# Bias rows of a modulation projection folded into its partial sums, and two of its chunks summed earlier

## The reference, cut to what matters

```
mod_l = split(silu(c) @ ada_w[i] + ada_b[i], 6)      # ada_w[i]: 1024 x 6144
h  = rmsnorm(x, norm_mix_g[i]) * (1 + mod_l[1]) + mod_l[0]
x  = x + mod_l[2] * mixer(h)
f  = rmsnorm(x, norm_ffn_g[i]) * (1 + mod_l[4]) + mod_l[3]
x  = x + mod_l[5] * grouped_moe(f)
```

## Time and profile before

| | us |
|---|---|
| three runs | 1031.48, 1037.86, 1030.33 (median 1031.48) |
| profiled execution | 1036.62, span of the trace 1034.8 |
| PE busy | 781.3 (76% of the span) |
| DVE busy | 392.3 (38%) |
| ACT busy | 178.6 (17%) |
| POOL busy | 28.0 (3%) |
| mean granted TensorE clock | 0.853 of full speed |

### The profile page before, as it was taken

How to read it: one execution, slowest core, us unless ns; L and a number is a source line. 1 busy time by engine, 2 the same in 40 slices (tenths; PEclk the granted TensorE clock), 3 DMA queues, 4 the chain that set the end, 5 groups by cost and what they waited for, 6 DMA issues and landing times.

```text
span 1034.8 us, 18303 instructions
## 1 busy us (share of the span) xinstructions
PE 781.3 (76%) x6820; PEld 433.2 (42%) x6821; DVE 392.3 (38%) x883; ACT 178.6 (17%) x381; POOL 28.0 (3%) x43
## 2 busy tenths in 40 slices
PE   3989899997959549976669953596478878798580
PEld 1534647544544225543235521272344444354240
DVE  2267879647978642120112101623512111121013
ACT  3211011115530201110111100420111111111001
POOL 0000000020000010000000001000000000000001
PEclk9899999799989669996779976799599898799785
DMA  9887988789507788589999899902789899999923
GB/s 346 297 300 254 343 296 286 274 303 320 213 1 269 302 342 346 215 350 415 418 417 414 337 416 396 404 20 102 294 307 365 325 416 417 414 417 415 415 82 127
DMA packets 102222, 320.53 MB, mean 310 GB/s; under 512 B 12315, under 2 KB 27547, under 8 KB 85667
## 3 DMA queue, kind: packets, MB, share of 16 engines
q1 hardware_dynamic: 78454, 282.88, 69.9%
q0 software_dynamic: 3952, 21.37, 5.4%
q10 hardware_dynamic: 19776, 15.75, 4.7%
HBM read 303.58 MB, written 24.64 MB: 317 GB/s over the span
## 4 chain that ended last, share of the span: by engine, by line
PE 30%; issue 27%; DVE 14%; DMA 13%; SPq 11%; ACT 1%; POOL 1%; ACTq 1%; DVEq 0%; POOLq 0%
PE bank L1469 7%; SPq L492 6%; DMA raw<-in_w_up 5%; DMA arena<-unit_rows 5%; PE bank L1678 3%; PE bank L1602 3%; PE bank L1785 3%; PE bank L1473 2%; DVE arena L873 2%; DMA arena<-in_ada_b 2%; PE bank L1691 2%; PE bank L1459 1%; PE bank L1478 1%; SPq L457 1%; DMA bias<-in_ada_b 1%
## 5 line engine op out<-in xcount | busy, mean ns | idle before, releaser
L1678 PE MATMUL bank<-raw,arena 128*32 128x256 f32 x3392 | 251.6, 441 | 73.2 <-DMA raw<-in_w_up 41.5
L1678 PEld LDWEIGHTS bank<-raw,arena 128*32 128x32 f32 x3392 | 120.5, 124 | 184.0 <-DMA raw<-in_w_up 57.1
L1285 DVE TENSOR_TENSOR arena<-arena,bank 64x256 f32<-64x256 f32 x53 | 22.5, 425 | 345.8 <-ACT arena L784 345.8
L1691 PE MATMUL bank<-raw,arena 128*32 128x256 f32 x1696 | 112.7, 393 | 0.8 <-DVE arena L1273 0.8
L1691 PEld LDWEIGHTS bank<-raw,arena 128*32 128x32 f32 x1696 | 60.8, 115 | 40.3 <-issue 5.6
L1469 PE MATMUL bank<-ring,arena 128*128 128x512 f32 x160 | 72.3, 611 | 0.0
L873 DVE SCALAR_TENSOR_TENSOR bias<-ring,small,bias 128x512 f32<-128x512 f32 x84 | 63.2, 752 | 3.0
L1665 PE MATMUL bank<-consts_sb,arena 64*128 64x64 f32 x212 | 37.0, 298 | 33.8 <-DVE arena L1285 17.2
L784 ACT ACTIVATE arena<-bank 64x256 f32<-64x256 f32 x53 | 19.9, 376 | 237.8 <-PE bank L1678 219.2
L1665 PEld LDWEIGHTS bank<-consts_sb,arena 64*128 64x128 f32 x212 | 29.4, 198 | 43.9 <-issue 23.6
L1469 PEld LDWEIGHTS bank<-ring,arena 128*128 128x128 f32 x160 | 31.2, 196 | 39.0 <-issue 39.0
(11 more groups left out here) (229 smaller groups left out, 792.5 us busy)
## 6 DMA issues: line engine op xcount, KB each, us to landing
raw<-in_w_gate SPq DMA_DIRECT2D x64, 1024.0 KB, 18.5
raw<-in_w_up SPq DMA_DIRECT2D x64, 1024.0 KB, 20.6
raw<-in_w_down SPq DMA_DIRECT2D x64, 1024.0 KB, 22.0
ring<-in_ada_w SPq DMA_DIRECT2D x24, 2048.0 KB, 13.3
ring<-in_w_in SPq DMA_DIRECT2D x7, 2048.0 KB, 10.9
unit_results<-arena ACTq DMA_DIRECT2D x244, 32.0 KB, 7.1
arena<-unit_rows ACTq DMA_DIRECT2D x55, 128.0 KB, 6.9
ring<-in_w_out SPq DMA_DIRECT2D x2, 2048.0 KB, 32.8
```

The source lines that it names most:

```text
L1678: ins = mm(ps[4][o:o + S, 0:FW], xT[:, i, j * S:(j + 1) * S], w[:, k % 4, h * FW:(h + 1) * FW], start=(k == 0), stop=(k == KD - 1))
L1691: ins = mm(ps[5][j * S:(j + 1) * S, 0:XW], hT_e[:, k % QN, k // QN * S:(k // QN + 1) * S], w[:, k % 2, j * XW:(j + 1) * XW], start=(k == 0 ...
```

## The change

The bias rows of layer 2's chunks are now loaded in the stream like those of layer 1, into a second two-row tile `bias1` that lies where the DFT constants go later, and every chunk's first pass starts from it. The three bias transfers and the three additions between the layers are gone. Chunks 20 and 21 are summed behind steps 21 and 22, ahead of the attention loop; 22 and 23 stay behind it. The fills stay behind chunk 19's save. At the passage, SP issues the three transfers of sums first, then the DFT constants (before: at the end of the stream), then waits for the results, and only then loads `w_fnet`. ACT makes eight of the twelve copies ahead of its squares and four behind them.

```diff
-ADA_AFTER = {n: 4 + i for i, n in enumerate((0, 2, 4, 5, 6, 7, 8, 9, 11, 12, 14, 16, 17, 18, 19, 20))}
-FILL_AFTER = 4 + len(ADA_AFTER) - 1
+ADA_AFTER = {n: 4 + i for i, n in enumerate((0, 2, 4, 5, 6, 7, 8, 9, 11, 12, 14, 16, 17, 18, 19, 20, 21, 22))}
+FILL_AFTER = 19
+MODS_FIRST = 8
+        bias1 = cst("dft").rearrange("p (b n) -> p b n", b=2)
...
             def load_bias(c):
                 if c >= 6:
                     sp.wait_ge(acc_ready, c - 5)
-                sp.dma_start(bias[0:1, c % 2, :], adab[0:1, c * W:(c + 1) * W]).then_inc(bias_in[c % 2], 16)
+                l, at = c // N_ADA, c % N_ADA * W
+                sp.dma_start((bias, bias1)[l][0:1, c % 2, :], adab[l:l + 1, at:at + W]).then_inc(bias_in[c % 2], 16)
...
-                if n and STREAM[n - 1][0] == "ada" and 4 <= STREAM[n - 1][1] < N_ADA:
+                if n and STREAM[n - 1][0] == "ada" and STREAM[n - 1][1] >= 4:
                     load_bias(STREAM[n - 1][1])
...
-            sp.dma_start(K_[:, K_PARTS[2]:K_PARTS[3]], consts[:, K_PARTS[2]:K_PARTS[3]]).then_inc(dft_in, 16)
...
-            sp.wait_ge(L[0]["expert_closed"], NE - 2)
+            sp.wait_ge(L[0]["expert_closed"], NE - 1)
+            for p in range(3):
+                sp.dma_start(mods[:, AT1[2 * p]:AT1[2 * p] + 2, :].rearrange("p a (b n) -> p (a b) n", b=2),
+                             scratch[4 * p:4 * p + 4].rearrange("c p n -> p c n")).then_inc(acc_back[p], 16)
+            sp.dma_start(K_[:, K_PARTS[2]:K_PARTS[3]], consts[:, K_PARTS[2]:K_PARTS[3]]).then_inc(dft_in, 16)
+            for t in range(TT):
+                sp.wait_ge(y_back[t], 32)
             for hf in range(2):
                 sp.dma_start(slot(FNET_AT + hf), fnet_v[:, :, hf * W:(hf + 1) * W]).then_inc(fnet_in[hf], 16)
-            sp.wait_ge(L[0]["expert_closed"], NE - 1)
-            for p in range(3):
-                load_sums(sp, p)
-            for t in range(TT):
-                sp.wait_ge(y_back[t], 32)
...
-            for n in range(N_ADA):
+            for n in range(MODS_FIRST):
                 mod1_copy(n)
             norm2(3, lambda t: act.wait_ge(added, t + 1))
+            for n in range(MODS_FIRST, N_ADA):
+                mod1_copy(n)
...
+            nc.vector.memset(bias1, 0.0).then_inc(bias_zero, 1)
...
                 for k in range(KD):
-                    if k == 0 and c >= N_ADA:
-                        ins = nc.vector.tensor_scalar(acc, w[:, k, :], cc[:, k:k + 1], None, ALU.mult)
-                    else:
-                        ins = nc.vector.scalar_tensor_tensor(acc, w[:, k, :], cc[:, k:k + 1],
-                                                             bias[:, c % 2, :] if k == 0 else acc, ALU.mult, ALU.add)
+                    first = (bias, bias1)[c // N_ADA][:, c % 2, :]
+                    ins = nc.vector.scalar_tensor_tensor(acc, w[:, k, :], cc[:, k:k + 1], first if k == 0 else acc,
+                                                         ALU.mult, ALU.add)
...
-                    if c < N_ADA:
-                        dve.wait_ge(bias_in[c % 2], 16 * (c // 2 - 1))
+                    dve.wait_ge(bias_in[c % 2], 16 * (c // 2 - 1))
...
-            for p in range(3):
-                add_bias1(p)
...
-                pe.wait_ge(bias1_added, c // 4 + 1)
                 pe.wait_ge(acc_back[c // 4], 16)
```

More of the change, by code:

```diff
@@ L339, in program @@
         gain_late = sem("gain_late")
-        bias1_added = sem("bias1_added")
-        acc_back, bias1_in = ([sem(f"{n}{p}") for p in range(3)] for n in ("acc_back", "bias1_in"))
+        acc_back = [sem(f"acc_back{p}") for p in range(3)]
         acc_saved = [sem(f"acc_saved{b}") for b in range(2)]
@@ L416, in program @@
         MOD1_ORDER = [2, 3, 0, 1] + list(range(4, N_ADA))
[L418 to L427, removed]
         @block.sync
@@ L466, in _ @@
                 if n == 4:
-                    sp.wait_ge(bias_zero, 1)
+                    sp.wait_ge(bias_zero, 2)
                     sp.dma_start(K_[:, K_PARTS[1]:K_PARTS[2]], consts[:, K_PARTS[1]:K_PARTS[2]]
@@ L857, in _ @@
             dve.wait_ge(silu_c, 1)
-            dve.wait_ge(bias_zero, 2)
+            dve.wait_ge(bias_zero, 3)
             nc.vector.tensor_tensor(c_pair[:, :, 0:2], cc.rearrange("p (w k) -> p k w", w=2),
@@ L1346, in combine_results @@
                     ins.then_inc(added, 1)
[L1348 to L1353, removed]
             residual(0, [0, 1, 2, 3], mod0[:, 0, :])
```

## The result

The changed kernel takes 1045.47 us (median of four runs, 1044.34 to 1046.18) against 1033.78 us for the kernel before (four runs, 1030.33 to 1037.86): ratio 1.0103, 95% interval 1.0076 to 1.0131. It is 11.7 us slower (1.0%). The forecast was +12.2 us and 1043.7 us, counted from 1031.48, the median of the three runs known then.

What follows compares the result with a forecast made beforehand. Serial chains were taken to bound the kernel: before the attention, and sums and biases between the layers. Terms 25.2 - 12.95 = +12.2 us on the median 1031.48 gave 1043.7 us, eight in ten from 1023 to 1052.

Steps and rivals of the forecast that it cites:

- The wait of chunk 21: Ahead of the attention: chunk 21's bias row, behind chunk 22's load, lands at 255.7; decay rows on DVE +25.2 us.
- Chunk 20: Ahead of the attention: its bias row follows chunk 21's load, so it runs from about 226.8 to 233.0.
- The rest of the stream at nothing: SP's other loads, held back one or two entries by the added bias rows, stay hidden: 0 us.
- Shorter work behind the attention and earlier weights at nothing: Behind the attention: two chunks fewer on DVE and 4 MB of expert weights sooner give 0 us.
- The passage: Between the layers: results fetch becomes the latest wait, DVE's mean at 650.7 instead of 663.65, -12.95 us.
- The total: Whole kernel: 25.2 - 12.95 = +12.2 us, for a median 1043.7 us; forecast as summed given 0.60.
- The rival with completion out of order: Ahead of the attention: chunk 21's row gets through the fills, 1021.0 us; chance 0.13 before 243, 0.10 to 252.

Runs made afterwards that it cites:

- the move alone: Kernel before with chunks 20 and 21 summed ahead of the attention, fills behind chunk 19's save, nothing folded, passage as before: 1033.89 us, ratio 1.0010.
- the variant with the rows first: Changed kernel with bias rows of chunks 20 and 21 issued just ahead of the loads of chunks 21 and 22: 1021.58 us, ratio 0.9909.

## Why the prediction was right, point by point

**The wait of chunk 21: right.** The row was taken to land 1.2 us ahead of chunk 22's load, at 255.7; it landed at 253.8, 2.1 us ahead of 255.9. Delay forecast +25.2, measured +23.3: the 1.9 us between them are the row's landing, 253.8 for 255.7, since the decay rows follow directly on chunk 21's sum. The cause was shown from three sides: the fills moved, the row moved, the packets made small. The one reading from which the row's landing was taken, 1.2 us ahead of its load, is not a fixed distance: rows landed 3.2 and 2.1 us ahead in the changed kernel, at least 3.2 with the fills moved and 5.0 with the fills in 2 KB runs. In a wait of 24 us this is small, and the forecast needed no more.

**Chunk 20: right.** Start forecast 226.8, found 223.3 with 3.1 us of waiting for its row. Chunk 21's load, ahead of the row, was in at 226.5 (issued at 215.4, in 11.1 us later), much as before (226.8); the row passed it by 3.2 us, where the forecast had given it no lead.

**The rest of the stream at nothing: right.** PE works through its projections without a new wait. The remark that `w_out` now waits for chunks 20 and 21 was made and then costed only for the order at hand; the same remark, carried one step on, would have foretold the variant with the chunks not moved. Of the experiments' expectations it is the one whose mechanism failed; several others missed a range or a size by up to 5 us, each said at its place.

**Shorter work behind the attention and earlier weights at nothing: right**, by the move alone, 1.0010 (0.9990 to 1.0031).

**The passage: right in size, -12.35 against -12.95.** Taking the same steps behind layer 2's experts as the price of an unhindered fetch gave 14.2 us, and 14.8 were found. What the forecast did not part was order and folding; the experiments give nearly all of it to the order.

**The clock: left out.** Between the two profiles it makes 3.1 us in the attention and the output map: +23.3 + 3.1 - 12.35 = +14.1, and with -1.2 of the transform (9.07 us where it was 10.25) +12.9, which is the +13.3 that stands at `w_fnet` but for the 0.4 within layer 1's experts. The 3.1 and the 1.2 us (7.4 to 10.2 in the other profiles) are, like the 3.8 of layer 2, within what these stretches differ by from one variant to the next, and no run ties them to the change.

**The total: right, and its closeness is luck.** The two terms of the forecast measured 23.3 - 12.35 = +10.95 us, against +12.2. The medians differ by 11.7, with an interval of about 8 to 13.5, and four executions of the kernel before lie 7.5 us apart. The half microsecond between forecast and medians says nothing.

**The rival with completion out of order: it did not come about here.** The row came 2.1 us ahead of the load it followed, where 12.5 us ahead would have been needed to turn the sign. That a row is in soon when only a load of 10 us is ahead of it is shown by the variant with the rows first. In every reading the row was in ahead of the load before it, but by 5.0 us at most.

## What to carry to other kernels

A transfer of 2 KB was late here by what stood ahead of it in its queue, and that by the packets of another queue. Before a wait on a small transfer is added, look at how long the large one issued just ahead of it takes to land, even if nobody has waited for it so far. Before folding a step away, try the order of the queue first: here the order alone hid the additions that the folding removed. And a wait that SP makes for one item holds everything behind it: list what stands behind it on the queue for each place the awaited work could have.

## What the runs showed of the hardware

- In stretches in which two DMA queues had work throughout, they moved nearly equal numbers of packets, whatever their sizes: 116 and 112 before, 89 and 91 after, 633 and 639 with the fills in 2 KB runs. In these stretches a copy from HBM to HBM of long contiguous rows had packets of 28 to 32 KB, one with runs of 2 KB had 3.6 KB. The share in bytes of the queue with 2 KB packets went from a fifteenth of the other's to more than half of it. That agrees with what the Trainium skill ("DMA: Bandwidth & Descriptors", Queues, rings and completion order) says of turns by packet.
- Issuing a 2 KB row took SP 21.0 us (229.57) while its queue stood still, where most such issues take 0.23 us; with the rows first the next one took 25.6 us (228.37). In this kernel a starved queue also held the engine that feeds it.
- Wherever the profiles let one read it, a 2 KB row landed ahead of the 2 MB load issued just before it: by 1.2 us in the kernel before, 3.2 and 2.1 in the changed kernel, 5.0 with the fills in 2 KB runs.
